# Last group of experts written out behind the loops, with two changes ahead of the experts

## What is computed

```python
m = adaln(cond, w_ada, b_ada)                 # silu(cond) @ w_ada + b_ada: 6 rows of 1024
h = modulate(rmsnorm(x, norm1_g), m, 0)
x = x + m[:, 2] * mixer(h)                    # attention and recurrent branch, merge, output projection
h = modulate(rmsnorm(x, norm2_g), m, 3)
# moe: sigmoid routing, top 8 of 64 experts for each token, gates
act = silu(h @ w_gate_e) * (h @ w_up_e) * gates
x = x + m[:, 5] * (sum_e(act @ w_down_e) + shared(h))
y = rmsnorm(x, final_g)
```

## Time and profile before

| | us |
|---|---|
| median of 3 runs | 969.09 |
| lowest and highest | 967.43 and 971.62 |
| the profiled execution's own time | 965.96 |
| its span, first to last instruction | 963.7 |
| busy PE, DVE, ACT, POOL | 883.8, 413.2, 253.4, 144.0 |
| read from HBM, mean over the span | 287.16 MB, 322 GB/s |

### The profile page before, as it was taken

How to read it: one execution, slowest core, us unless ns; L and a number is a source line. 1 busy time by engine, 2 the same in 40 slices (tenths; PEclk the granted TensorE clock), 3 DMA queues, 4 the chain that set the end, 5 groups by cost and what they waited for, 6 DMA issues and landing times.

```text
span 963.7 us, 12124 instructions
## 1 busy us (share of the span) xinstructions
PE 883.8 (92%) x4170; PEld 514.4 (53%) x4170; DVE 413.2 (43%) x947; ACT 253.4 (26%) x415; POOL 144.0 (15%) x213
## 2 busy tenths in 40 slices
PE   4799998999999999999997999999999999999973
PEld 2387875899897764543333444444443444444431
DVE  1562483577665554233331332432342334233445
ACT  2537623344423240221211111111111111111111
POOL 7300000000001041122132012012102111111112
PEclk9799999999999999999998999999999999999987
DMA  9974778422227197799999999999999999999832
GB/s 341 343 252 182 293 262 239 109 89 79 98 89 297 64 415 316 243 340 390 404 388 386 421 403 400 410 403 394 423 404 398 404 420 401 402 406 414 340 107 101
DMA packets 85320, 295.65 MB, mean 307 GB/s; under 512 B 17370, under 2 KB 33814, under 8 KB 60320
## 3 DMA queue, kind: packets, MB, share of 16 engines
q1 hardware_dynamic: 64400, 263.21, 68.7%
q0 software_dynamic: 12176, 27.37, 10.0%
q10 hardware_dynamic: 8704, 4.54, 2.1%
HBM read 287.16 MB, written 22.81 MB: 322 GB/s over the span
## 4 chain that ended last, share of the span: by engine, by line
PE 67%; DMA 19%; DVE 5%; issue 3%; ACT 2%; SPq 2%; POOL 1%; ACTq 1%; POOLq 0%; DVEq 0%
PE bank L1466 21%; DMA gu<-in_w_up_e_dram 12%; PE bank L1485 10%; PE bank L1090 7%; PE bank L1092 6%; PE bank L1091 6%; DMA y_dram<-y_sb,slot_row 4%; DMA chunk_raw<-in_w_ada_dram 3%; PE bank L1503 3%; PE bank L1454 3%; PE bank L1118 2%; PE bank L1359 2%; PE bank L1159 1%; PE bank L1192 1%; PE bank L1541 1%
## 5 line engine op out<-in xcount | busy, mean ns | idle before, releaser
L1466 PE MATMUL bank<-gu,x_t 128*64 128x512 f32 (+1 forms) x1024 | 286.4, 601 | 12.8 <-DMA gu<-in_w_up_e_dram 11.0
L1466 PEld LDWEIGHTS bank<-gu,x_t 128*64 128x64 f32 (+1 forms) x1024 | 102.6, 151 | 167.7 <-issue 162.2
L1485 PE MATMUL bank<-dn,a_t 128*64 128x512 f32 (+1 forms) x512 | 145.3, 597 | 4.1 <-ACT shared_sb L1016 3.5
L1985 DVE TENSOR_TENSOR act_sb<-silu_sb,bank 128x256 f32<-128x256 f32 x40 | 16.9, 422 | 229.4 <-ACT silu_sb L1059 229.4
L1059 ACT ACTIVATE silu_sb<-bank 128x256 f32<-128x256 f32 x40 | 15.4, 385 | 330.0 <-PE bank L1466 330.0
L748 POOL DMA_INDIRECT y_dram<-y_sb,slot_row x27 | 45.9, 1701 | 306.5 <-DVE slot_row L1875 260.6
L1485 PEld LDWEIGHTS bank<-dn,a_t 128*64 128x64 f32 (+1 forms) x512 | 48.5, 150 | 74.0 <-issue 67.4
L1090 PE MATMUL bank<-h_hi,chunk_lo 128*128 128x384 f32 x240 | 84.6, 353 | 0.0
L1092 PE MATMUL bank<-h_hi,chunk_hi 128*128 128x384 f32 x240 | 81.1, 338 | 0.0
L1091 PE MATMUL bank<-h_lo,chunk_hi 128*128 128x384 f32 x240 | 81.0, 337 | 0.0
L736 POOL DMA_INDIRECT xg<-h_dram,slot_tok x42 | 44.0, 1047 | 179.8 <-DVE slot_row L1875 155.5
(11 more groups left out here) (345 smaller groups left out, 1072.7 us busy)
## 6 DMA issues: line engine op xcount, KB each, us to landing
gu<-in_w_gate_e_dram SPq DMA_DIRECT2D x64, 1024.0 KB, 15.7
gu<-in_w_up_e_dram SPq DMA_DIRECT2D x64, 1024.0 KB, 20.8
dn<-in_w_down_e_dram SPq DMA_DIRECT2D x64, 1024.0 KB, 26.0
chunk_raw<-in_w_ada_dram SPq DMA_DIRECT2D x24, 1024.0 KB, 8.9
chunk_raw<-in_w_in_dram SPq DMA_DIRECT2D x18, 1024.0 KB, 5.4
chunk_raw<-in_w_out_dram SPq DMA_DIRECT2D x4, 1024.0 KB, 5.0
y_dram<-zeros POOLq DMA_DIRECT2D x1, 3072.0 KB, 17.6
chunk_raw<-in_w_pa_dram SPq DMA_DIRECT2D x2, 1024.0 KB, 5.0
```

What stands on the lines that cost most here:

```text
L1466: mm = pe.matmul(bank[2 + u % 2][at_x, :].rearrange("p (g n) -> p g n", g=2), x_t[:, cols], wide[:, :, k, :], start=(k == 0), stop=(k == K ...
L1485: mm = pe.matmul(bank[5 + half][at_x, :], a_t[:, cols], dn[slot_of(x, first)][:, wc], start=(k == 0), stop=(k == 1))
```

## The change

1. **Opening.** Chunks 0 to 7 hold 2 parts of K for all 1024 columns (4 KB runs). Both halves of a row are complete with the fourth chunk. DVE copies one half, ACT the other.
2. **gate_ffn.** POOL keeps the row in `m_late`. Its four spreading products and four copies go from ahead of the output projection into turn 4 of the first group. Turn 5's gate and up products wait for the first copy, its token transposes for all four.
3. **Last group.** The loops run two groups, and the last group is written out with `last=True`. In it the blocks 0, 2, 8 and 9 (`ENDING`) are placed and 5 and 7 are scattered, so that 28 scatters are made instead of 27 and the last is that of block 7. SP waits for that one. Work for blocks behind the last (gathers, transposes, numbers) is left out. `acc_add` gates and adds `ffn_acc` in turns 5, 6 and 7. `place_ending` puts block 8's products ahead of block 9's down products (which go to banks 3 and 7) and adds block 9's to the same banks. `sums_add` adds the loaded sums on DVE.

```diff
-                if kind == "ada":
+                if kind == "ada" and i < 8:
+                    a, c = divmod(i, 4)
+                    sp.dma_start(dst[:, :].rearrange("p (k n) -> p k n", k=2),
+                                 w_ada[0].rearrange("(p k) n -> p k n", k=KD)[:, 2 * c:2 * c + 2, D * MODS[a]:D * MODS[a] + D]).then_inc(loaded, 16)
...
-            sp.wait_ge(S["added"], passes * (NGRP * SCATTERED * 16) + 16 * (len(PLACED) - 1))
+            sp.wait_ge(S["added"], passes * (NGRP * SCATTERED * 16) + 16 * len(PLACED))
...
+            for a in range(2):
+                act.wait_ge(S["ada_mm"], 4 * a + 4)
+                act.activation(m_row[a % 2][:, 512:1024], bank[7][:, :], ACT.Copy).then_inc(S["ada_row"], 1)
...
-            spread_copy(1, gate_ffn, 1.0)
             split_high(act, number[("out", 1)])
...
-            pe.wait_ge(S["merge_gated"], 2 * KD - 4)
-            spread(1)
             pe.wait_ge(S["hl_ready"], 1)
             pe.wait_ge(S["merge_gated"], 2 * KD)
             pe.transpose(bank[6][0:8, 0:P], h_last[:, :], ident[:, :]).then_inc(S["hl_mm"], 1)
-            pe.wait_ge(S["bc_evac"], 8)
...
+                pe.wait_ge(S["a_ready"], b * UN + UN)
+                pe.wait_ge(S["place_made"], ahead(1) + 2)
+                pe.wait_ge(S["y_half"], ahead(1) + 1)
+                for n in range(3):
+                    product(n, 0, y_hi, start=True)
...
+                down(UN - 1, b, False, (bank[3], bank[7]))
+                pe.wait_ge(S["y_half"], ahead(1) + 2)
+                for n in range(3):
+                    product(n, 1, y_hi)
+                pe.wait_ge(S["y_ready"], b * UN + UN)
+                for n in range(3, 6):
+                    product(n, 1, y_hi)
...
+                    if first and u == SPREAD_TURN:
+                        pe.wait_ge(S["late_row"], 1)
+                        pe.wait_ge(S["x_first"], i + 2)
+                        pe.wait_ge(S["x_second"], i + 2)
+                        pe.wait_ge(S["a_ready"], i + 1)
+                        for n in range(4):
+                            spread(n, spread_bank(n), m_late)
...
-            with pe.Fori(1, passes * NGRP) as b:
+            with pe.Fori(1, passes * NGRP - 1) as b:
                 block_turn(b, False)
...
+            block_turn(passes * NGRP - 1, False, True)
...
+                if last:
+                    sums_add(0)
+                    sums_add(1)
+                    for half in range(2):
+                        ending_low(b, 1, half)
+                    sums_add(2)
+                    ending_sums(b)
...
+            def sums_add(t):
+
+                dve.wait_ge(S[first_half[t][0]], first_half[t][1] + 16)
+                dve.wait_ge(rows_loaded[t], 32)
+                go(dve.tensor_tensor(ffn[t][:, :], ffn[t][:, :], ffn_b[t][:, :], ALU.add))
+                go(dve.tensor_tensor(ffn[t][:, :], ffn[t][:, :], gate_ffn[:, int(t > 0), :], ALU.mult))
+                go(dve.tensor_tensor(x_sb[:, t, :], x_sb[:, t, :], ffn[t][:, :], ALU.add))
```

More of the change, by code:

```diff
@@ L409, in hybrid_step, with placed_in, is_placed, scatters_ahead @@
         assert max(PLACED) < UN - 2 and all(v + 1 not in PLACED for v in PLACED)
[L411 to L414 removed]
+        assert len(ENDING) == len(PLACED) and {SLOT[x] for x in turns[False][UN - 3]} == {1, 2}
+        assert not {SLOT[x] for u in (UN - 2, UN - 1) for x in turns[False][u]} & {1, 2}
+        def placed_in(last):
+            return ENDING if last else PLACED
+        def is_placed(u, first, last=False):
+            return not first and u % UN in placed_in(last and u >= 0)
+        def scatters_ahead(b, u, last=False):
             back = 1 if u < 0 else 0
[L417 to L421 removed]
+            here = placed_in(last and not back)
+            return b * (16 * SCATTERED) + 16 * (len(PLACED) - SCATTERED * back + sum(v not in here for v in range(u % UN)))
+        def places_ahead(b, v, each, last=False):
+            return b * (each * len(PLACED)) + each * (placed_in(last).index(v) - len(PLACED))
         def place_outs(u):
@@ L762, in block_turn @@
                         count(tok_no[:, :], [[1, NTOK]], 0).then_inc(S["zero_filled"], 1)
-                    if not (first and u == 0) and not (u and is_placed(u - 1, first)):
-                        scatter(i - 1, u - 1, 16 * (i - 1) if first else scatters_ahead(b, u - 1))
+                    if not (first and u == 0) and not (u and is_placed(u - 1, first, last)):
+                        scatter(i - 1, u - 1, 16 * (i - 1) if first else scatters_ahead(b, u - 1, last))
             gather(0, 0)
@@ L1469, in gate_up, with down @@
                             mm.then_inc(S["gu_used"], 1)
-            def down(u, b, first):
+            def down(u, b, first, outs=(bank[5], bank[6])):
                 experts = turns[first][u]
@@ L1489, in down, with place @@
                                 mm.then_inc(S["dn_half"], 1)
-            def place(v, b):
+            def place(v, b, last=False):
                 i, at_y = b * UN + v, v % 2
+                ahead = lambda each: places_ahead(b, v, each, last)
                 outs = place_outs(v + 1)
@@ L1608, in _ @@
             for a in range(2):
-                for h in range(2):
-                    row(a, h)
+                dve.wait_ge(S["ada_mm"], 4 * a + 4)
+                row(a, 0)
                 mod_sum(a)
@@ L1986, in block_turn @@
                                       ALU.mult).then_inc(S["act_ready"], 1)
-                    x_copy(i + 1)
-                    placing = u and is_placed(u - 1, first)
+                    if not last or u + 1 < UN:
+                        x_copy(i + 1)
+                    ending = last and u == UN - 1
+                    placing = u and is_placed(u - 1, first, last) and not ending
+                    if ending:
+                        for n in range(2):
+                            ending_matrix(n)
+                        ending_low(b, 0, 0)
                     if placing:
                         place_matrix(u - 1)
-                        place_low(u - 1, b, 0)
+                        place_low(u - 1, b, 0, last)
                     dve.wait_ge(S["at_mm"], i + 1)
```

265 lines of the change are left out of this document (158 added, 107 removed).

## The result

| | kernel before | changed kernel |
|---|---|---|
| median of the first comparison | 968.26 us (4 runs, the first three among them) | 949.67 us (4 runs, 947.81 to 950.78) |
| second series | 964.89 us (9 runs) | 948.82 us (5 runs) |
| third series | 965.88 us (9 runs) | 950.65 us (5 runs) |
| the profiled execution's own time, and span | 965.96, 963.7 us | 948.58, 946.8 us |

The first comparison gives a ratio of 0.9831 with a 95% interval of 0.9807 to 0.9854, the later ones 0.9840 (0.9811 to 0.9869) and 0.9844 (0.9827 to 0.9860). The change makes the kernel 15 to 16 us faster.

A forecast was written before the change was run, and what follows sets the result against it. The prediction took loads to bound the opening and the experts, with PE close behind. Terms -1.1 - 4.0 + 0 - 8.2 = -13.3 us took 969.09 to 955.8 us, range 952 to 962.

The forecast's parts named there:

- Opening loads: Opening: 4 KB runs load the eight modulation chunks faster, -1.1 us, bounds 0 and 1.7, nothing else added.
- rival (c): Turn 9 without slow clock, opening loads at upper bound: 954.0, or 952.5 if opening clock stays up; 0.62 together with forecast.
- gate_ffn out of the merge: Ahead of the output projection: without the four products and their copies it starts earlier, -4.0 us, bounds -3.6 and -4.1.
- gate_ffn in turn 4: First expert group: the queue of loads, 6.4 us, covers up to 4.6 us of added PE time; 0, bounds 0 and +4.6.
- (a): First expert group: the moved spreading is not hidden by the load queue, 4.6 us return, 960.4 us; chance 0.15.
- (d): Experts: the earlier start does not carry, the load stream ends when it did, 5.1 us lost, 960.9 us; chance 0.08.
- The last group: Last turns to last addition: PE skips two placings, turn 9 starts sooner, DVE's sums end at 945.1 against 953.3, -8.2 us.
- Rival (b): End: successive scatters run late, so the loaded sums come 3 to 4 us later, 959.5 us; chance 0.12.
- Rival (e): Last group: the scatter chain holds back ACT's buffers and PE's down products, 969 us or more; 0.03 with other losses.
- From the execution to the median: Whole kernel: the median lies 3.1 us above the profiled execution, so the sum was applied to 969.09 us.

The follow-up runs named there:

- runs2k: Changed kernel with its opening chunks loaded in 2 KB runs again, each chunk in two transfers: 956.44 us (6 runs).
- fills: Changed kernel with repeated or unused transposes filling PE's opening waits, and 16 transposes each ahead of gate and up in the last group's turns 7 and 9: 947.67 us.
- late_start: Kernel before, its 2 KB loads kept, with PE's first modulation products also waiting for the fourth chunk: 963.44 us against 965.65, ratio 0.9970.
- early_cond: Changed kernel with the biases' small load on its own semaphore, so ACT's silu and PE's first products no longer wait for it: 950.72 us (5 runs).
- open_only: Kernel before with only the opening part of the change (4 KB runs, new product order, copies split with ACT): 963.06 us against 965.03, ratio 0.9991.
- open_merge: Kernel before with the first two parts of the change (opening loads, gate_ffn moved to turn 4), last group as it was: 958.85 us, ratio 0.9944.
- hold: Kernel before with PE held ahead of the second row's first modulation products until that row's third chunk is loaded: 965.47 us (8 runs).
- fill_after: Changed kernel with transposes filling PE's waits in the opening only (ahead of the last chunk's products, the row's transposes and the first projection): 947.35 us (4 runs).
- fills_again: The kernel of fills measured once more, beside the changed kernel in the same series: 946.27 us against 950.65 (5 runs each), ratio 0.9804.
- last_only: Kernel before with only the third part of the change, the written-out last group: 960.50 us against 965.65, ratio 0.9924.

## Why the prediction was wrong

**Opening loads (-1.1): right in the loads, wrong in what hangs on them.** The last chunk's products came at 28.50, as forecast 28.5, and runs2k shows that the run length does it. The step that failed is the one that ends the term there ("Taken: -1.1", upper bound 1.7): it treated the rest of the opening as unchanged. The mark moved by 3.85 us in the profile and, over ten executions with 4 KB runs (63.3 to 65.3, mean 64.0) and three with 2 KB runs and PE's work as before (65.6, 67.2, 67.6, mean 66.8), by 2.8. The prediction named the clock of the opening as "another 1.5 if the clock in the opening stays up" in rival (c), with no rows for it and outside the sum; in the pair of profiles the clock gave 2.7. The earlier trace rows held the sign: the last chunk's eight products took 1.94 us where those at the full clock take 1.07. That PE's pauses matter to the clock is shown by the fills: no fall from 20 to 48 us in the three profiles of the changed kernel with fills, one in each of the ten profiles with 4 KB runs and no fills there. That PE's order alone can move a fall to a place where it costs nothing is shown by late_start. Why the fall mostly comes later with 4 KB runs, even with PE's early start (early_cond), is open.

**gate_ffn out of the merge (-4.0): right.** 4.1 in the profile, 4.2 between the medians of open_only and open_merge.

**gate_ffn in turn 4 (0): right, with less room than said.** The shift was 4.5 us at the first turn of group 1 (508.28 to 503.78) and 8.6 again in the last group. Cover is 5.0 us and not 6.4. The wait of 5.61 us shrank to 3.42 and not to 1: PE came to it 4.5 us earlier, and the load behind it not 8.7 but only 6.7 (519.27 instead of 525.95). The stream had the rest back by the last group; what held it there was not tried. Rivals (a) and (d) fall.

**The last group (-8.2): right, in part because errors cancelled.** Turn 9 started at 902.53, which is 911.1 in the clock of the kernel before (shift 8.6), forecast 910.4; the two waits for loads were 2.65 and 2.06 us, forecast 2 to 4; DVE's row was 20.5 us without a gap, forecast 21.4. The end was forecast at 45.1 (span's end 955.5 without the shifts ahead of it, less 910.4); thirteen profiled executions with the third part gave 43.5 to 46.3, by how far the clock fell in turn 9. In the first profile it did not fall there, where the forecast had put 1.2 us; against that stand 0.7 for the later start of the turn, 0.7 for the longer way to the first sum (0.59 of it the wait for the loaded sums) and 0.5 for a tail of 10.9 us instead of 10.4; DVE's shorter row gave 0.9. Rival (b) is half there: DVE waited 0.59 us for the loaded sums, where the forecast had 0.9 to spare; 11 of the 13 profiles with the third part have no such wait. Rival (e), the slower side, did not show: no wait of PE hangs on a scatter in the last group.

**From the execution to the median (+3.1): wrong.** This is the second step that failed, and the larger. The sum was put on the 969.09 of three runs. In the five later series the kernel before had 964.9 to 965.9, and the profiled execution's own 965.96 was already there. From 965.4 the forecast would have been 952.1. So 3.7 of the 6.1 us are this step, and 2.4 the change itself: 1.7 the opening (2.8 for 1.1), the rest within what the medians spread. In the two later series the change was 16.1 and 15.2 us, where the forecast had 13.3.

## What to carry to other kernels

Where PE's products in a stage with waits take longer than the same products elsewhere, price that clock as a term of its own: an edit that moves the waits will move it, and here it was worth more than the loads (2.7 us in the pair of profiles, 1.7 in the mean of all, against 1.1). Idle time of PE ahead of such a place may be filled with products into a free bank, or PE may start later and work in one row; both are a line or two. The fills took 3.9 us off over all runs, the later start 2.2 off the kernel before. Work put under a queue of loads is free only up to what the queue holds (some 5 us here), however long PE's later waits for loads add up to be, and a median of three runs is too few to build a forecast of 1% on.

## What had not been expected of the hardware

- The length of a load's runs reaches the small loads beside it: with 4 KB runs the biases let ACT go at 16.9 to 17.4 us, with 2 KB runs at 12.8 to 13.2.
- The clock's fall in the opening is movable. By the stretches of 4 us it stood from 28 to 44 us (before), from 24 to 32 and 36 to 44 (hold), from 20 to 24 and 36 to 40 (late_start), from 32 to 40 (changed kernel), and nowhere from 20 to 48 us in fill_after, fills and fills_again.
- It also moves by itself: the third execution of the changed kernel had it from 28 to 44 us (mark 65.29), and three of the 19 profiles, open_only, last_only and early_cond, have one between 328 and 352 us in the routing, which the other 16 do not show. It made the way from the mark to the experts 4 to 9 us longer. In early_cond it covers most of the 8.7 us between the profiled execution and the median; much of the spread between executions may come from such falls, but only profiled executions show them.
- An addition on DVE with both inputs in SBUF took 3.27 instead of 1.22 us beside an operation of POOL, which itself took 3.33 for what DVE does in 1.23, 1.1 of it while DVE's operation ahead was still running.
